# Moving the split weights' tiles by 448 bytes inside the on-chip memory

## The reference

```python
def swiglu(h, w_gu, w_down):
    a, b = jnp.split(h @ w_gu, 2, axis=-1)
    return (jax.nn.silu(a) * b) @ w_down
...
        h2 = _rms_norm(x, g_pre_mlp[l])
        m = jnp.square(jax.nn.relu(h2 @ w_up[l])) @ w_down[l]
        x = x + _rms_norm(m, g_post_mlp[l])
```

## The kernel before

| tile | first byte | modulo 128 | modulo 512 |
|---|---|---|---|
| `raw` | 16,512 | 0 | 128 |
| `w_hi` | 41,088 | 0 | 128 |
| `w_lo` | 53,376 | 0 | 128 |
| `cst` (constants: identity, masks) | 65,664 | 0 | 128 |
| `cols` (gains and biases as columns, 440 bytes) | 72,448 | 0 | 256 |
| `z_hi`, `z_lo` | 102,592 and 110,784 | 64 | 192 |
| `h_hi`, `h_lo` | 163,520 and 179,904 | 64 | 192 |
| `n_hi`, `n_lo` | 212,672 and 220,864 | 64 | 192 |

## Time and profile before

### The profile page before, as it was taken

How to read it: one execution, slowest core, us unless ns; L and a number is a source line. 1 busy time by engine, 2 the same in 40 slices (tenths; PEclk the granted TensorE clock), 3 DMA queues, 4 the chain that set the end, 5 groups by cost and what they waited for, 6 DMA issues and landing times.

```text
span 821.0 us, 14292 instructions
## 1 busy us (share of the span) xinstructions
PE 795.5 (97%) x5493; PEld 693.6 (84%) x5493; DVE 429.1 (52%) x684; ACT 418.8 (51%) x641; POOL 377.1 (46%) x181
## 2 busy tenths in 40 slices
PE   5999999999899999999999999999999999999996
PEld 3778877887777999999998889999887988899985
DVE  4675569984566533332336747645456333423435
ACT  5335426455846444544444855654756544444443
POOL 3126000000164654566545986564464555666452
PEclk9999999999999999999999999999999999999999
DMA  9984567223943656555654796434455456566541
GB/s 321 310 274 138 162 240 245 59 97 109 358 148 106 205 182 202 179 179 184 195 167 134 224 208 180 130 107 132 148 171 164 157 183 196 180 193 189 188 146 51
DMA packets 94396, 146.61 MB, mean 179 GB/s; under 512 B 15741, under 2 KB 64110, under 8 KB 94352
## 3 DMA queue, kind: packets, MB, share of 16 engines
q1 hardware_dynamic: 92896, 143.23, 54.7%
q0 software_dynamic: 1424, 2.77, 1.2%
q10 hardware_dynamic: 32, 0.01, 0.0%
HBM read 144.93 MB, written 1.06 MB: 178 GB/s over the span
## 4 chain that ended last, share of the span: by engine, by line
PE 84%; DVE 6%; issue 3%; DMA 2%; POOL 2%; ACT 2%; SPq 0%; DVEq 0%; ACTq 0%; POOLq 0%
PE bank L1878 82%; POOL w_lo L629 2%; DMA raw<-in_w_mod 2%; PE bank L2148 1%; ACT w_hi L694 1%; DMA gate_mlp_b<-gate_rows 1%; PE bank L2456 1%; DVE x L1830 1%; DVE w_lo L1197 1%; DVE stat L1514 1%; DVE x L1643 0%; DVE o_lo L1735 0%; DVE bank L1642 0%; DVE probs L1474 0%; DVE hg_queries L1384 0%
## 5 line engine op out<-in xcount | busy, mean ns | idle before, releaser
L629 POOL TENSOR_TENSOR w_lo<-raw,w_hi 128x1024 fp32r<-128x1024 f32 (+2 forms) x150 | 362.0, 2429 | 318.4 <-ACT w_hi L694 318.2
L694 ACT ACTIVATE w_hi<-raw 128x1024 fp32r<-128x1024 f32 (+1 forms) x218 | 226.2, 1045 | 214.6 <-PE bank L1878 190.8
L1197 DVE TENSOR_TENSOR w_lo<-raw,w_hi 128x1024 fp32r<-128x1024 f32 x71 | 87.2, 1239 | 139.5 <-ACT w_hi L694 139.3
L1878 PE MATMUL bank<-z_hi,w_hi 128*128 128x256 f32 x384 | 108.8, 283 | 0.1
L1878 PE MATMUL bank<-z_hi,w_lo 128*128 128x256 f32 x384 | 107.4, 280 | 0.0
L1878 PE MATMUL bank<-z_lo,w_hi 128*128 128x256 f32 x384 | 107.1, 279 | 0.0
L1878 PE MATMUL bank<-n_hi,w_hi 128*128 128x256 f32 x352 | 98.6, 280 | 1.1 <-POOL w_lo L629 1.0
L1878 PE MATMUL bank<-n_hi,w_lo 128*128 128x256 f32 x352 | 98.4, 280 | 0.0
L1878 PE MATMUL bank<-n_lo,w_hi 128*128 128x256 f32 x352 | 98.1, 279 | 0.0
L1878 PE MATMUL bank<-w_hi,mlp_h_hi 128*128 128x512 f32 x216 | 85.6, 396 | 0.0
L1878 PE MATMUL bank<-w_lo,mlp_h_hi 128*128 128x512 f32 x216 | 85.4, 395 | 0.0
(11 more groups left out here) (419 smaller groups left out, 1554.7 us busy)
## 6 DMA issues: line engine op xcount, KB each, us to landing
raw<-in_w_in SPq DMA_DIRECT2D x54, 512.0 KB, 4.5
raw<-in_w_down SPq DMA_DIRECT2D x54, 512.0 KB, 3.6
raw<-in_w_gu SPq DMA_DIRECT2D x44, 512.0 KB, 3.5
raw<-in_w_up SPq DMA_DIRECT2D x32, 512.0 KB, 3.7
raw<-in_w_mod SPq DMA_DIRECT2D x24, 512.0 KB, 4.0
raw<-in_w_mod SPq DMA_DIRECT2D x32, 256.0 KB, 5.9
raw<-in_w_out SPq DMA_DIRECT2D x12, 512.0 KB, 3.8
raw<-in_w_in SPq DMA_DIRECT2D x8, 336.0 KB, 3.1
```

What stands on the lines that cost most here:

```text
L629: nc.gpsimd.tensor_tensor(wl[:, w % SPL, 0:size], raw[:, slot_raw, 0:size], wh[:, w % SPL, 0:size].bitcast(F32), ALU.subtract).then_inc(s_ ...
L694: nc.scalar.activation(wh[:, w % SPL, 0:size], raw[:, slot_raw, 0:size], ACT.Copy).then_inc(s_hi, 1)
L1197: V.tensor_tensor(wl[:, w % SPL, :], raw[:, slot_raw, :], wh[:, w % SPL, :].bitcast(F32), ALU.subtract).then_inc(s_lod, 1)
L1878: return nc.tensor.matmul(out_, l, r_, start=start, stop=stop, skip_group_check=True)
```

## The change

`cols`, 440 bytes in each partition and rounded up to 448, is named before `w_hi` instead of behind `cst`. So `w_hi`, `w_lo` and `cst` start 448 bytes higher, at 41,536, 53,824 and 66,112 (all 64 modulo 128 and 64 modulo 512), and `cols` starts at 41,088. `raw`, everything from `b_gate_cols` on and the total size stay as they are. No instruction is added, removed or moved on any engine, and no size, wait or transfer is another; only the addresses of four tiles are.

```diff
         raw = sb("raw", [P, RAW, CHUNK])
+        cols = sb("cols", [P, R_N])
         wh = sb("w_hi", [P, SPL, CHUNK], F32R)
         wl = sb("w_lo", [P, SPL, CHUNK], F32R)
         cst = sb("cst", [P, C_N])
-        cols = sb("cols", [P, R_N])
         bgc = sb("b_gate_cols", [P, 16])
```

## The result

| | before | after |
|---|---|---|
| median, same chip | 821.27 us (820.99 to 821.56, 9 runs) | 826.07 us (824.46 to 830.21, 9 runs) |
| profiled execution | 822.76 us | 825.59 us |
| its span | 821.0 us | 823.8 us |
| granted clock | 0.997 | 0.999 |

The ratio is 1.0059, with an interval of 1.0047 to 1.0072: slower by 0.6%, where I forecast no change. 826.07 lies inside the range of 810 to 834.

The account below looks back on a forecast made before the run. It took back-to-back matmuls on PE (795.5 of 821.0 us busy) as the bound; all address terms were 0, so the sum of 0 left the median of 821.3 us, no change at 0.48, range 810 to 834.

Parts of the forecast that it names:

- The place of one against the other: Matmuls with split weights: the weights' address relative to the activations' was taken to cost 0, bounded by 15.6 gained, 17.2 lost.
- the borders between two runs: Second MLP, where runs of 256 and 512 columns meet: single pairs at equal places modulo 128 showed usual pitches, hence 0.
- a sweeping distance: Within each matmul the stream passes 1024 bytes per 512-byte weight load, so 64 bytes at the start should wash out: 0.
- faster rival: Matmul streams: the new distance of 128 bytes avoids a clash and the long pitch falls away; 805.7 us in full, chance 0.22.
- a whole step: Gap between two pitches of the same matmul stream: 4.2 ns for 256 columns, 4.6 ns for 512.
- slower rival: Matmul streams: stream and load meet in the same 128-byte half, finishing one step later; 838.5 us in full, chance 0.21.
- a third pitch: Matmul pitch absent from the trace of before, named as what would make the prediction wrong; no size given.
- The two read ports: Skill's independent matrix engine ports, by which address changes are worth nothing; 109 and 216 ns estimated, not leaned on.
- The place itself: Weights as matmul operands: their own address modulo 128, apart from the activations', was taken to cost 0.
- The splitting engines: DVE, ACT and POOL computing `w_hi` and `w_lo`: 0 taken, POOL's 10% is 1.2 us; chance 0.02 faster, 0.02 slower.
- The short stretches: Runs with the shorter pitch before: some 170 matmuls of 256 columns at 113.5 ns, all 192 streaming `h` at 229.2.
- the small form of the slower rival: Only the short stretches fall into the long pitch: 1.6 us, 822.9 us; chance 0.05 with a little more.

Follow-up runs that it names:

- m1: Small program of matmuls alone on zeros, 256 columns, operand starts varied in 64-byte steps, 64 runs of 24; 113.3 to 120.0 ns per matmul.
- e4: Kernel before, with the split weights moved to 256 modulo 512, 64 bytes above the activations; 810.84 us, ratio 0.9874.
- m2: The same small program as m1 with 512 columns instead of 256; 226.7 to 233.3 ns per matmul.
- e2: Kernel before, with `w_hi`, `w_lo` and `cst` moved up by 512 bytes, `cols` and `b_gate_cols` in front; 821.41 us, ratio 1.0003.
- e6: Changed kernel, with the activations of both blocks moved to 128 modulo 512, so all distances are those of before; 821.5 us, ratio 1.0001.
- e7: Kernel before, weights not moved, all split activations up by 64 bytes, giving the changed kernel's distance of 128; 823.82 us, ratio 1.0032.
- e1: Kernel before, with `cst` moved to 64 modulo 512 behind `cols`, the weights left at 128; 820.92 us, ratio 1.0001.
- e9: e4, with stationary tiles of both MLPs' hidden values and `merged` up by 64 bytes, distance 0 for 512 columns of streamed weights; 816.1 us, ratio 0.9932.
- m3: The same small program as m1, 256 columns, with operand starts in steps of 32 bytes; no distance below 113.3 ns.
- e8: The changed kernel run once more without an edit, for a second trace and time; 824.46 us, ratio 1.0038.

## Why the prediction was wrong

**The place of one against the other costs 0: this step failed.** The prediction took 0 from the borders between two runs, where a single pair at equal places follows "within the rounding of the rows", and from an argument that a sweeping distance washes a shift out. The argument is refuted by m1: 64 bytes change the pitch of a stream by up to 6.7 ns, of 512 columns too. The borders were the wrong rows. A pitch settles only after several matmuls. In m1 the run at distance +128 goes on after its first step with 119, 112, 117, 123 and 120 ns, the one at +256 with 118, 125, 113 and 119 and only then 120 throughout. e4's first five at 118 ns and the following 43 at 113.3 show the same in the kernel. A single matmul, of 0.11 us in rows rounded to 0.01, can't show 1 or 2 ns, nor the rhythm that a run of 48 at that distance would find. I chose the rows that resembled the new layout in their addresses and not those that resembled the work in the length of the run.

**The right row was in the text, under a rival.** The faster rival names it: 512 columns of `h` at 229.2 against 512 columns of `w` at 233.8, with nothing different but the roles of the two operands and so the sign of the distance. That was a whole step between two distances in runs of 24, with all 192 of `h` on one side, and the argument against it (the same tiles run at 113.5 and 117.7) does not touch it. That argument was true, but its reading was wrong: m1 has 13 runs at 117.8 and 3 at 113.3 for -64. The distance narrows down the rhythms (never 113.3 at 0 or 128 in m1), but at one distance more than one can last.

**The size.** The slower rival had the direction, but neither its mechanism nor its size held. It let stream and load meet because both start in the same half of 128 bytes; distances of 0 and 128 bytes both do that, and with 512 columns they have 227.4 and 232.6 ns in m2's means. And it added one whole step, 4.2 ns, where the new distance has a pitch of its own, +1.2 and +1.9 ns. The text named "a third pitch" as what would make it wrong, and 118.7 and 120.0 are third pitches. For 512 columns its step of 4.6 ns had the wrong sign, -1.0 ns. With the measured pitches the sum is 2,652 x 1.6 + 192 x 2.8 - 1,139 x 0.8 ns = 4.2 + 0.5 - 0.9 = 3.8 us, 825.1 on the old median. That 826.07 lies in the range is no merit of the forecast: the range was made wide by the two rivals, and the forecast of no change had a range of its own of 820.0 to 822.6. From the rows of before alone the direction could not be had, since the distance of 128 bytes doesn't occur in them. A measured map could have given it: m1's mean of 118.6 against 116.9 ns makes 2,652 x 1.7 = 4.5 us of loss for 256 columns.

**The two read ports.** m1 and m2, with no other engine at work on their operands, have 113.3 to 120.0 ns for 256 columns and 226.7 to 233.3 for 512, by the starts of the operands alone. The Trainium skill (TensorE: Matmul & The Clock Gate, Part 2) has two independent read ports, and columns / 2.4 + 2.5 ns between matmuls, by which the estimates are 109 and 216 ns; it calls this the isolated gap and says that in a stream of weight loads and matmuls both set the spacing. The traces do not agree with the formula, which has no addresses in it. Whether two reads disturb each other, no run here shows. The prediction did not lean on the page, but its own argument led to the same 0.

**What was right.** The place itself costs 0, though not for the reason given: the price of 256 columns more, taken as 116.1 ns and equal for both streams, goes from 107.6 to 120.0 with the distance (m1, m2). e2 shows the 0 for 512 bytes, e6 for the change's own 448 with the distance restored (1.0001, 0.9991 to 1.001), e7 from the other side. The splitting engines kept their durations within 1%. `cst` costs 0 (e1). The difference is the pitch times the number of matmuls, as the working has it. The short stretches did fall into a longer pitch, as the small form of the slower rival has it. For `h` with 512 columns that is 2.8 ns in the mean and not 4.6, 0.5 us. Those of 256 columns, 152 steps in six stretches, run at 118.4 to 120.0 ns after, more than 4.2 ns longer, and take 0.8 us more, part of the sum above.

## What to carry to other kernels

Where a kernel is bound by back-to-back matmuls, each with new weights, the distance between its stationary and its streamed operand, modulo 256 bytes, is a tuning knob that costs no instruction: here, with fp32r, it was worth -10.5 us or +4.8 us of 821. Measure it with a small map of long runs for each shape of matmul that the kernel has, since the best distance for 256 columns is not that for 512, and sum over all shapes before choosing. Judge by the pitch over whole runs, not by borders or by recorded durations, and time the whole kernel, since a run can carry on in a slower rhythm that the run ahead of it left. Before two traces are compared, compare their granted clocks stretch by stretch: here a slow stretch in the trace of before hid 1.6 of the 3.8 us that the pitches cost.

## What the runs showed of the hardware

- The pitch of fp32r matmuls follows the difference between the starts of the two operands, not either start, with a period of 256 bytes: 113.3 to 120.0 ns for 256 columns, 226.7 to 233.3 for 512 (m1, m2). The sign counts: with 512 columns +64 has 233.3 in all 16 runs and -64 has 228.9 in all; with 256 columns +64 has 113.3 in 15 of 16 runs and -64 has 117.8 in 13 of 16.
- For 512 columns the order is another: 0 is best (226.7 to 228.1) and +64 worst (233.3). 256 columns more cost between 107.6 ns (distance 0) and 120.0 ns (+64), the differences of the two maps' columns.
- At one distance several rhythms can last: 113.3 and 117.8 at +64 (e4 against e9, a whole run of 48 in each; m3, four runs each), the same two at -64 (m1: 3 and 13 runs), 118.8 and 120.0 in one loop of one program (e8 and the first trace of after). What picks one of them outside the loops is open.
- The granted clock adds a spread of its own. The first 9 runs of the changed kernel spread over 5.8 us, and the two slowest, 828.11 and 830.21, have the lowest clocks, 0.993 and 0.994; the three at 0.998 and 0.999 took 824.46 to 825.59. The runs of before beside e6 to e9 spread over 4.3 us; their ten at 0.999 took 820.21 to 821.23, where e8's one at 0.999 took 824.43. So the loss stands at an equal clock too. How much of the slowest runs is clock and how much a longer rhythm is open, as they have no trace.
- In one such stretch, 3.5 us at a granted clock of 0.51, matmuls took about twice as long from start to start and 1.6 us were lost (the trace of before, from 218.6 us); the trace of after has 1.00 there.
- Steps inside a lasting rhythm need not be equal: at +128 they repeat 118, 122, 120, 119, 115; at 0 they are 120 throughout, at +64 113 and 114 (m1).
- What in the engine or the memory makes the distance count is open. No run here tells a clash of two reads from another cause with the same period.
